# Splitting the right operands of a Strassen-style matmul kernel two k-tiles at a time

## The chip, the cores and the metric

The kernel runs on one core of a Trainium2 chip (trn2). The core's engines each work through a queue of their own, in order, and meet at semaphores: TensorE (PE) does the matmuls, VectorE (DVE) and ScalarE (ACT) the elementwise work, GpSimd (POOL) a little at the start, SyncE (SP) issues the transfers. The metric is the device time of one execution in microseconds (us), median of the runs shown.

## What is computed

One layer on x of 1024 rows by 1024 features, all in float32: a gated mixer and a squared-ReLU MLP, each behind an RMS norm and with a residual.

```python
def gmlp_mixer(h, w_in, ln_g, w_s, b_s, w_out):
    z = jax.nn.gelu(h @ w_in)                     # 1024 -> 4096
    u, v = jnp.split(z, 2, axis=-1)
    ...                                           # layer norm of v, times ln_g
    v = v.reshape(b, l // CHUNK, CHUNK, GM_GROUPS, GM_GDIM)
    ws = jnp.where(causal[None], w_s, jnp.zeros_like(w_s))
    sv = jnp.einsum('gts,bnsge->bntge', ws, v) + b_s.T[None, None, :, :, None]
    return (u * sv.reshape(b, l, GM_WIDTH)) @ w_out

x = x + gmlp_mixer(rms_norm(x, norm1_g), ...)
x = x + jnp.square(jax.nn.relu(rms_norm(x, norm2_g) @ mlp_w1)) @ mlp_w2
return rms_norm(x, final_g)
```

## The kernel before

**Stages.** Every large product is cut into products of 1024x1024 by 1024x1024, and each of these is done by Strassen's scheme with seven products of 512x512 blocks instead of eight. Eight *single* stages n = 0 to 7 make the two v halves (n = 0, 1), the two u halves (2, 3) and the four parts of the MLP's hidden layer (4 to 7). Three *double* stages d = 0 to 2 take two such products at once into the same sums: w_out after stage 3, w2 after stage 7. A stage has seven positions, one for each product. The right operands are weight blocks b11 to b22, loaded as they are, or differences of them (T1 to T4, made by DVE at L1228 with `sum_t`).

**Split numbers.** A float32 operand is split into a high part (rounded to the fast type fp32r, by ACT) and a low part (the rest, by DVE), and a product is three matmuls: high by high, low by high, high by low (`products`, L387, L391, L392). A *unit* is one k-tile (128 of the 512 terms) of one position: 12 matmuls, three for each of four PSUM banks.

**The ring.** The left operands' parts stay in SBUF for the whole stage. The right operands' parts pass through a ring of four slots. In a single stage a slot holds one k-tile: `ring_high` and `ring_low`, each 128x512. `split_high` (L855) rounds a k-tile on ACT, once PE has finished the unit that had the slot; `split_low` (L1192) subtracts on DVE. The semaphores `high_done` and `low_done` count k-tiles, and PE waits for `low_done` before each unit. In a double stage a slot holds the left and the right operand of a unit, 128x1024 each of high and low: `pair_high` (L883), `pair_low` (L1200). Its first two slots lie where the ring's four lie, the other two in another region.

**Order.** The order on each engine is written out by hand in `single(n)` and `double(d)`: the four splits of every position are set down one at a time, and the other work stands between them: sums of the results in PSUM (`add_block`, L1309, four operations of 128x512), the T differences, sums for the next stage's left operand (`sum_s`, L1418), evictions and activations on ACT, and in stages 2 and 3 (the u halves) the gating. Gating a block takes a layer norm on ACT (`normalise`, L1001), 16 products of 128x128 in each of which the fp32 matmul runs as two (`mini`, L443) on PE, and eight operations on DVE (`gate`, L1357 and L1372). The names matter at position 5 of stages 2 and 3, where DVE's part of the order is:

```python
                split_low(n, 5, 0)
                split_low(n, 5, 1)
...
                if kind(n) == "u":
                    gate(n, "c11")
                sum_t(n, 3)
                split_low(n, 5, 2)
                if kind(n) == "u":
...
                    nc.vector.tensor_tensor(block_of["c12"], block_of["c12"], block_of["c22"], ALU.add)\
                      .then_inc(p5_added, 1)
                split_low(n, 5, 3)
```

The 128x2048 sum in it is L1523. At the end of a stage the first splits of the next one (`next_high`, `next_low`) stand between the last gates: the gate for c22 ahead of the third, the gate for c12 ahead of the fourth. In stage 1, two copies of the transposed gating weights (`ws_t`, L1496) follow the fourth split of position 3, and PE needs the banks that they empty within that position.

Of the kernel before, what the change touches and what calls it, by code (L numbers as in the profile page):

```python
# [5 lines left out]
F32 = mybir.dt.float32  # L6
F32R = mybir.dt.float32r
# [50 lines left out]
def unit(n, pos, k):  # L58

    return 4 * (7 * n + pos) + k + (56 if n >= 4 else 0)  # L60
# [56 lines left out]
def trunk(nc, x, norm1_g, norm2_g, mlp_w1, mlp_w2, final_g, a_w_in, a_ln_g, a_ws, a_bs, a_w_out, out):  # L117
# [8 lines left out]
    with ExitStack() as ctx:  # L126
        def at(name, shape, offset, dt=F32):
            return nc.alloc_sbuf_tensor_at(name, shape, dt, offset=offset)
# [49 lines left out]
        block_of = {"c11": rows[:, 0:4, 0:NB], "c12": rows[:, 0:4, NB:], "c21": rows[:, 4:8, 0:NB],  # L178
                    "c22": rows[:, 4:8, NB:]}

        ring_high = [at(f"ring_high{e}", [P, NB], ring_at + 4096 * e, F32R) for e in range(4)]
        ring_low = [at(f"ring_low{e}", [P, NB], ring_at + 4096 * e + 2048, F32R) for e in range(4)]
        pair_at = [ring_at, ring_at + HALF, region("a12"), region("a12") + HALF]
        pair_high = [at(f"pair_high{e}", [P, 2, NB], pair_at[e], F32R) for e in range(4)]
        pair_low = [at(f"pair_low{e}", [P, 2, NB], pair_at[e] + 4096, F32R) for e in range(4)]
# [193 lines left out]
        def _(pe):  # L379
# [6 lines left out]
            def products(bank, stat_high, stat_low, mov_high, mov_low, start, stop, begins):  # L386
                first = nc.tensor.matmul(ps[:, bank, :], stat_high, mov_high, start=start, stop=False,  # L387
                                         skip_group_check=True)
                if begins:
                    first.then_inc(unit_begun, 1)  # L390
                nc.tensor.matmul(ps[:, bank, :], stat_high, mov_low, start=False, stop=False, skip_group_check=True)  # L391
                last = nc.tensor.matmul(ps[:, bank, :], stat_low, mov_high, start=False, stop=stop,  # L392
                                        skip_group_check=True)
                if stop:
                    last.then_inc(full[bank], 1)

            def single_unit(n, pos, k):
                s = S_SINGLE[pos]
                if n in (0, 4):
                    if pos == 0:  # L400
                        pe.wait_ge(combo_low, (10 if n == 4 else 0) + k + 1)
                    elif k == 0:
                        pe.wait_ge(combo_low, combo_low_count(n, s))
                pe.wait_ge(low_done, unit(n, pos, k) + 1)
                e = k % 4
                for m in range(4):
                    bank = set_of(slot(n, pos))[m]
                    if k == 0:
                        begin_fill(("product", n, pos), bank)
                    c = slice(m * P, (m + 1) * P)  # L410
                    starts = pos in CHAIN_START or (pos == 5 and kind(n) == "u")
                    start, stop = k == 0 and starts, k == 3
                    if kind(n) == "v":
                        products(bank, high[s][:, k, c], low[s][:, k, c], ring_high[e][:, :], ring_low[e][:, :],
                                 start, stop, m == 0)
                    else:
                        products(bank, ring_high[e][:, c], ring_low[e][:, c], high[s][:, k, :], low[s][:, k, :],
                                 start, stop, m == 0)

            def double_unit(d, pos, k):  # L420
# [401 lines left out]
        def _(act):  # L822
# [12 lines left out]
            def right_place(n, pos):  # L835
                return quarter[places(n)[{0: "b11", 1: "b21", 2: "b21", 3: "b11", 4: "b12", 5: "b22", 6: "b21"}[pos]]]

            def split_high(n, pos, k):
                if pos == 7:
                    n, pos = n + 1, 0  # L840
                u = unit(n, pos, k)
                if u == 0:
                    act.wait_ge(first_landed, 16)
                else:
                    right_ready(n, pos)
                if n == 4 and pos == 0 and k < 2:
                    act.wait_ge(unit_begun, done(unit_double(0, 6, 6)))
                elif n == 4 and pos == 0:
                    filled(act, ("double", 0, 6), set_of(slot_double(0, 6))[3])
                elif u >= 4 and k < 3:  # L850
                    act.wait_ge(unit_begun, done(u - 4))
                elif u >= 4:
                    before = (n, pos - 1) if pos else (n - 1, 6)
                    filled(act, ("product", *before), set_of(slot(*before))[3])
                nc.scalar.activation(ring_high[k][:, :], right_place(n, pos)[:, k, :], ACT.Copy)\  # L855
                  .then_inc(high_done, 1)

            def split_pair_high(d, pos, k):
                if pos == 7:
# [316 lines left out]
        def _(dve):  # L1176
# [8 lines left out]
            def right_place(n, pos):  # L1185
                return quarter[places(n)[{0: "b11", 1: "b21", 2: "b21", 3: "b11", 4: "b12", 5: "b22", 6: "b21"}[pos]]]

            def split_low(n, pos, k):
                if pos == 7:
                    n, pos = n + 1, 0  # L1190
                dve.wait_ge(high_done, unit(n, pos, k) + 1)
                nc.vector.tensor_tensor(ring_low[k][:, :], right_place(n, pos)[:, k, :],  # L1192
                                        ring_high[k][:, :].bitcast(F32), ALU.subtract).then_inc(low_done, 1)

            def split_pair_low(d, pos, k):
                if pos == 7:
# [513 lines left out]
```

## Time and profile before

| | before |
|---|---|
| median of 3 runs | 1149.25 us (1149.21 to 1150.16) |
| the profiled execution | 1149.28 us, span of its profile 1147.6 us |
| PE busy | 1126.0 us, 98% |
| DVE busy | 773.2 us, 67% |
| ACT busy | 561.4 us, 49% |
| granted TensorE clock, mean | 0.994 |

The span runs from the first to the last instruction of the profile; times in its views count from its start. An engine's busy time is a sum over stages; what it hides is seen in the waits of the engine that is busy nearly always, here PE, and in the order of time around them. In a timeline an entry in brackets gives the idle time of the engine before the row and the instruction that ended it.

### The profile page before, as it was taken

How to read it: one execution, taken by the hardware profiler on the slowest of the kernel's cores; microseconds unless marked ns; L12 is line 12 of the kernel's file. 1: busy time of each engine (PE TensorE's matmuls, PEld its weight loads, DVE VectorE, ACT ScalarE, POOL GpSimd, SP SyncE). 2: the span in 40 equal slices, each digit the busy share in tenths (PEclk: the TensorE clock that was granted, in tenths of full speed). 3: DMA queues.
4: the chain of work that ended last, by engine and by line, in shares of the span. 5: the costliest groups of instructions: out<-in, count | busy, mean ns of one | idle time of the engine just before them, and what ended most of it. 6: DMA issues, size and time to landing. Idle time of an engine off the chain costs nothing.

```text
span 1147.6 us, 13154 instructions
## 1 busy us (share of the span) xinstructions
PE 1126.0 (98%) x5155; PEld 937.4 (82%) x5155; DVE 773.2 (67%) x830; ACT 561.4 (49%) x855; POOL 19.6 (2%) x16
## 2 busy tenths in 40 slices
PE   9999999999999999999999999999999999999995
PEld 8888888888888788888888888888887888888884
DVE  6886655478678976657657547465587675676666
ACT  8663434553553334656664365455643343434443
POOL 5000000000000000000000000000000000000000
PEclk9999999999999999999999999999999999999998
DMA  8054253272965493331353635527858454242313
GB/s 330 1 183 147 74 184 110 74 251 80 330 236 205 167 334 142 146 111 37 110 184 115 216 111 194 195 107 275 293 220 304 153 203 183 110 177 80 110 37 146
DMA packets 74621, 191.17 MB, mean 167 GB/s; under 512 B 3104, under 2 KB 4160, under 8 KB 67904
## 3 DMA queue, kind: packets, MB, share of 16 engines
q1 hardware_dynamic: 74496, 190.33, 46.2%
q8 instruction: 40, 0.66, 0.2%
q14 instruction: 21, 0.17, 0.0%
q10 hardware_dynamic: 64, 0.02, 0.0%
HBM read 131.61 MB, written 58.72 MB: 166 GB/s over the span
## 4 chain that ended last, share of the span: by engine, by line
PE 88%; DVE 5%; issue 2%; DMA 2%; ACT 2%; POOL 1%; DVEq 0%; SPq 0%; ACTq 0%; POOLq 0%
PE banks L387 28%; PE banks L391 28%; PE banks L392 28%; PE banks L443 2%; DVE pair_low L1200 1%; POOL rows L1675 1%; DMA rows<-y_blocks 1%; PE banks L479 1%; DVE left_and_right L1249 1%; PE banks L450 1%; DMA rows<-in_x_dram 1%; DVE rows L1632 1%; DVE rows L1332 1%; DVE rows L1372 0%; ACT spare L1012 0%
## 5 line engine op out<-in xcount | busy, mean ns | idle before, releaser
L883 ACT ACTIVATE pair_high<-left_and_right 128x1024 fp32r<-128x1024 f32 x168 | 177.6, 1061 | 268.0 <-PE banks L387 215.5
L1192 DVE TENSOR_TENSOR ring_low<-left_and_right,ring_high 128x512 fp32r<-128x512 f32 x224 | 152.6, 689 | 214.5 <-ACT ring_high L855 214.1
L1200 DVE TENSOR_TENSOR pair_low<-left_and_right,pair_high 128x1024 fp32r<-128x1024 f32 x168 | 203.0, 1220 | 122.5 <-ACT pair_high L883 122.4
L855 ACT ACTIVATE ring_high<-left_and_right 128x512 fp32r<-128x512 f32 x224 | 139.4, 630 | 272.8 <-PE banks L387 174.7
L387 PE MATMUL banks<-pair_high 128*128 128x512 f32 x672 | 263.2, 392 | 3.4 <-DVE pair_low L1200 3.3
L391 PE MATMUL banks<-pair_low,pair_high 128*128 128x512 f32 x672 | 262.4, 390 | 0.0
L392 PE MATMUL banks<-pair_high,pair_low 128*128 128x512 f32 x672 | 262.1, 390 | 0.0
L387 PEld LDWEIGHTS banks<-pair_high 128*128 128x128 f32 x672 | 126.5, 188 | 31.3 <-DVE pair_low L1200 4.5
L387 PE MATMUL banks<-s_high,ring_high 128*128 128x512 f32 x384 | 149.6, 390 | 0.0
L391 PE MATMUL banks<-s_low,ring_high 128*128 128x512 f32 x384 | 149.5, 389 | 0.0
L392 PE MATMUL banks<-s_high,ring_low 128*128 128x512 f32 x384 | 149.5, 389 | 0.0
L392 PEld LDWEIGHTS banks<-pair_high,pair_low 128*128 128x128 f32 x672 | 126.6, 188 | 26.4
L391 PEld LDWEIGHTS banks<-pair_low,pair_high 128*128 128x128 f32 x672 | 126.6, 188 | 25.8
L387 PE MATMUL banks<-a_high,ring_high 128*128 128x512 f32 x288 | 112.8, 392 | 0.6 <-DVE scratch L1357 0.5
L392 PE MATMUL banks<-a_high,ring_low 128*128 128x512 f32 x288 | 112.2, 389 | 0.0
L391 PE MATMUL banks<-a_low,ring_high 128*128 128x512 f32 x288 | 112.1, 389 | 0.0
L392 PEld LDWEIGHTS banks<-s_high,ring_low 128*128 128x128 f32 x384 | 72.1, 188 | 15.0
L391 PEld LDWEIGHTS banks<-s_low,ring_high 128*128 128x128 f32 x384 | 72.1, 188 | 14.8
L387 PEld LDWEIGHTS banks<-s_high,ring_high 128*128 128x128 f32 x384 | 72.1, 188 | 14.8
L1228 DVE TENSOR_TENSOR left_and_right<-left_and_right 128x2048 f32<-128x2048 f32 x32 | 73.1, 2286 | 1.1
L387 PEld LDWEIGHTS banks<-a_high,ring_high 128*128 128x128 f32 x288 | 54.1, 188 | 12.4 <-DVE scratch L1357 1.5
L392 PEld LDWEIGHTS banks<-a_high,ring_low 128*128 128x128 f32 x288 | 54.1, 188 | 11.3
(101 smaller groups left out, 1213.1 us busy)
## 6 DMA issues: line engine op xcount, KB each, us to landing
left_and_right<-sums SPq DMA_DIRECT2D x40, 1024.0 KB, 7.3
left_and_right<-in_mlp_w_dram SPq DMA_DIRECT2D x36, 1024.0 KB, 6.3
sums<-rows SPq DMA_DIRECT2D x34, 1024.0 KB, 5.0
left_and_right<-in_a_w_in_dram SPq DMA_DIRECT2D x19, 1024.0 KB, 6.3
v_blocks<-rows SPq DMA_DIRECT2D x8, 1024.0 KB, 4.8
left_and_right<-in_a_w_out_dram SPq DMA_DIRECT2D x8, 1024.0 KB, 11.0
spare<-v_blocks SPq DMA_DIRECT2D x6, 1024.0 KB, 5.8
sums<-spare SPq DMA_DIRECT2D x6, 1024.0 KB, 3.9
```

Source lines behind the costliest of these rows:

```text
L387: first = nc.tensor.matmul(ps[:, bank, :], stat_high, mov_high, start=start, stop=False, skip_group_check=True)
L391: nc.tensor.matmul(ps[:, bank, :], stat_high, mov_low, start=False, stop=False, skip_group_check=True)
L392: last = nc.tensor.matmul(ps[:, bank, :], stat_low, mov_high, start=False, stop=stop, skip_group_check=True)
L443: mm = nc.tensor.matmul(ps[:, banks[m], c * P:(c + 1) * P], held[:, c, m * P:(m + 1) * P], ws_t[:, g, :], start=True, stop=True)
L450: nc.tensor.matmul(ps[:, 0, 0:P], ident[:, :], ident[:, :], start=True, stop=True)
L479: tr = nc.tensor.transpose(ps[:, banks[k], c * P:(c + 1) * P], rows[:, 4 * tb + c, f:f + P], ident[:, :])
L855: nc.scalar.activation(ring_high[k][:, :], right_place(n, pos)[:, k, :], ACT.Copy)\
L883: nc.scalar.activation(pair_high[(k + 2) % 4][:, :, :], pair_of(d, pos, k), ACT.Copy)\
L1192: nc.vector.tensor_tensor(ring_low[k][:, :], right_place(n, pos)[:, k, :], ring_high[k][:, :].bitcast(F32), ALU.subtract).then_inc(low_don ...
L1200: nc.vector.tensor_tensor(pair_low[e][:, :, :], pair_of(d, pos, k), pair_high[e][:, :, :].bitcast(F32), ALU.subtract).then_inc(low_done, 1)
L1228: nc.vector.tensor_tensor(*args, ALU.subtract).then_inc(t_summed, 1)
L1249: nc.vector.tensor_tensor(*args, ALU.subtract).then_inc(t_summed, 1)
```

## The change

In the single stages the right operand is rounded and subtracted for two k-tiles at once, in one 128x1024 operation on each engine, and the ring becomes two pairs in the tiles that the double stages use. A pair is made at the place in the order where its second k-tile was made (k odd); the call for the first k-tile does nothing any more. `high_done` and `low_done` go up by two. Only the very first position (stage 0, position 0) keeps single k-tiles. ACT's wait before a pair is the one that the second k-tile had. The double stages aren't touched.

```diff
-        ring_high = [at(f"ring_high{e}", [P, NB], ring_at + 4096 * e, F32R) for e in range(4)]
-        ring_low = [at(f"ring_low{e}", [P, NB], ring_at + 4096 * e + 2048, F32R) for e in range(4)]
         pair_at = [ring_at, ring_at + HALF, region("a12"), region("a12") + HALF]
...
             def single_unit(n, pos, k):
                 s = S_SINGLE[pos]
+                right_high, right_low = pair_high[k // 2][:, k % 2, :], pair_low[k // 2][:, k % 2, :]
...
-                        products(bank, high[s][:, k, c], low[s][:, k, c], ring_high[e][:, :], ring_low[e][:, :],
+                        products(bank, high[s][:, k, c], low[s][:, k, c], right_high, right_low,
                                  start, stop, m == 0)
...
             def split_high(n, pos, k):
...
+                first = (n, pos) == (0, 0)
+                if k % 2 == 0 and not first:
+                    return
                 u = unit(n, pos, k)
...
                 elif u >= 4:
                     before = (n, pos - 1) if pos else (n - 1, 6)
                     filled(act, ("product", *before), set_of(slot(*before))[3])
-                nc.scalar.activation(ring_high[k][:, :], right_place(n, pos)[:, k, :], ACT.Copy)\
-                  .then_inc(high_done, 1)
+                if first:
+                    nc.scalar.activation(pair_high[k // 2][:, k % 2, :], right_place(n, pos)[:, k, :], ACT.Copy)\
+                      .then_inc(high_done, 1)
+                else:
+                    nc.scalar.activation(pair_high[k // 2][:, :, :], right_place(n, pos)[:, k - 1:k + 1, :], ACT.Copy)\
+                      .then_inc(high_done, 2)
...
             def split_low(n, pos, k):
...
+                if k % 2 == 0 and not first:
+                    return
                 dve.wait_ge(high_done, unit(n, pos, k) + 1)
...
+                else:
+                    nc.vector.tensor_tensor(pair_low[k // 2][:, :, :], right_place(n, pos)[:, k - 1:k + 1, :],
+                                            pair_high[k // 2][:, :, :].bitcast(F32), ALU.subtract)\
+                      .then_inc(low_done, 2)
```

How the order on DVE changes, at the two kinds of places that the prediction speaks of. Names: `ring_low_79` to `_82` are the four slots, `pair_low_79` and `_80` the two pairs; line numbers after the diff are 15 higher, or 14 for the subtraction.

DVE in stage 2, from the second split of position 5 to the `add_block` after its last, before:

```order
L1192 TENSOR_TENSOR ring_low_80<-left_and_right,ring_high_76 128x512
L1357 SCALAR_TENSOR_TENSOR scratch<-banks,gains,bias 128x512 x2
L1372 TENSOR_TENSOR rows<-scratch,rows 128x512
L1357 SCALAR_TENSOR_TENSOR scratch<-banks,gains,bias 128x512
L1372 TENSOR_TENSOR rows<-scratch,rows 128x512
L1357 SCALAR_TENSOR_TENSOR scratch<-banks,gains,bias 128x512
L1372 TENSOR_TENSOR rows<-scratch,rows 128x512 x2
L1228 TENSOR_TENSOR left_and_right<-left_and_right 128x2048
L1192 TENSOR_TENSOR ring_low_81<-left_and_right,ring_high_77 128x512
L1523 TENSOR_TENSOR rows<-rows 128x4x512
L1192 TENSOR_TENSOR ring_low_82<-left_and_right,ring_high_78 128x512
L1309 TENSOR_TENSOR rows<-banks,rows 128x512 x4
```

and now:

```order
L1206 TENSOR_TENSOR pair_low_79<-left_and_right,pair_high_75 128x1024
L1372 SCALAR_TENSOR_TENSOR scratch<-banks,gains,bias 128x512 x2
L1387 TENSOR_TENSOR rows<-scratch,rows 128x512
L1372 SCALAR_TENSOR_TENSOR scratch<-banks,gains,bias 128x512
L1387 TENSOR_TENSOR rows<-scratch,rows 128x512
L1372 SCALAR_TENSOR_TENSOR scratch<-banks,gains,bias 128x512
L1387 TENSOR_TENSOR rows<-scratch,rows 128x512 x2
L1243 TENSOR_TENSOR left_and_right<-left_and_right 128x2048
L1538 TENSOR_TENSOR rows<-rows 128x4x512
L1206 TENSOR_TENSOR pair_low_80<-left_and_right,pair_high_76 128x1024
L1324 TENSOR_TENSOR rows<-banks,rows 128x512 x4
```

The third k-tile's subtraction, which stood ahead of the large sum, is now part of the one behind it.

DVE in stage 1, position 3, around the copies of the gating weights, before:

```order
L1192 TENSOR_TENSOR ring_low_81<-left_and_right,ring_high_77 128x512
L1228 TENSOR_TENSOR left_and_right<-left_and_right 128x2048
L1192 TENSOR_TENSOR ring_low_82<-left_and_right,ring_high_78 128x512
L1496 COPY ws_t<-banks 128x512 x2
L1192 TENSOR_TENSOR ring_low_79<-left_and_right,ring_high_75 128x512
```

and now:

```order
L1206 TENSOR_TENSOR pair_low_79<-left_and_right,pair_high_75 128x1024
L1243 TENSOR_TENSOR left_and_right<-left_and_right 128x2048
L1206 TENSOR_TENSOR pair_low_80<-left_and_right,pair_high_76 128x1024
L1511 COPY ws_t<-banks 128x512 x2
L1206 TENSOR_TENSOR pair_low_79<-left_and_right,pair_high_75 128x1024
```

Ahead of the copies a subtraction of 128x512 has become one of 128x1024.

## Rows read from the trace of the kernel before

**Rows 1.** The page: busy time, share of the span and instructions of each engine.

```profile
PE 1126.0 (98%) x5155; PEld 937.4 (82%) x5155; DVE 773.2 (67%) x830; ACT 561.4 (49%) x855; POOL 19.6 (2%) x16
```

**Rows 2.** The page's groups: count, busy us, mean ns of one, idle before.

```profile
L883 ACT ACTIVATE pair_high<-left_and_right 128x1024 fp32r<-128x1024 f32 x168 | 177.6, 1061 | 268.0 <-PE banks L387 215.5
L1192 DVE TENSOR_TENSOR ring_low<-left_and_right,ring_high 128x512 fp32r<-128x512 f32 x224 | 152.6, 689 | 214.5 <-ACT ring_high L855 214.1
L1200 DVE TENSOR_TENSOR pair_low<-left_and_right,pair_high 128x1024 fp32r<-128x1024 f32 x168 | 203.0, 1220 | 122.5 <-ACT pair_high L883 122.4
L855 ACT ACTIVATE ring_high<-left_and_right 128x512 fp32r<-128x512 f32 x224 | 139.4, 630 | 272.8 <-PE banks L387 174.7
```

**Rows 3.** PE's waits: for whom, us in total, times, longest.

```profile
PE banks L387 <- DVE pair_low L1200: 3.3, 3, 2.1
PE banks L479 <- POOL rows L1675: 2.2, 1, 2.2
PE banks L443 <- ACT spare L1001: 1.6, 1, 1.6
```

**Rows 4.** Timeline of DVE, stage 2, position 5: start, duration, row.

```profile
229.98 0.69 DVE L1192 TENSOR_TENSOR ring_low<-left_and_right,ring_high 128x512 fp32r<-128x512 f32 x1 [5.25 <-ACT ring_high L855]
230.59 1.40 DVE L1357 SCALAR_TENSOR_TENSOR scratch<-banks,gains,bias 128x512 f32<-128x512 f32 x2
...
236.01 2.29 DVE L1228 TENSOR_TENSOR left_and_right<-left_and_right 128x2048 f32<-128x2048 f32 x1
...
238.82 2.29 DVE L1523 TENSOR_TENSOR rows<-rows 128x2048 f32<-128x2048 f32 x1
241.02 0.68 DVE L1192 TENSOR_TENSOR ring_low<-left_and_right,ring_high 128x512 fp32r<-128x512 f32 x1
```

**Rows 5.** Timelines of ACT and PE there: second rounding, third k-tile's first matmul.

```profile
229.31 0.63 ACT L855 ACTIVATE ring_high<-left_and_right 128x512 fp32r<-128x512 f32 x1 [5.31 <-PE banks L387]
...
239.72 0.39 PE L387 MATMUL banks<-s_high,ring_high 128*128 128x512 f32 x1
```

**Rows 6.** The same of a common place, stage 6, position 5, first pair.

```profile
724.00 0.63 ACT L855 ACTIVATE ring_high<-left_and_right 128x512 fp32r<-128x512 f32 x1 [2.09 <-PE banks L387]
...
728.95 0.39 PE L387 MATMUL banks<-s_high,ring_high 128*128 128x512 f32 x1
```

**Rows 7.** Chain, PE's timeline, and windows: stretch, length, PE busy (count), clock, DMA.

```profile
882.37 1.14 DVE pair_low L1200
...
883.55 0.73 PE L387 MATMUL banks<-pair_high 128*128 128x512 f32 x1 [2.12 <-DVE pair_low L1200]
...
30.30:33.70 3.40, 3.40 (x18) 0.50 0.00 0
...
365.10:368.50 3.40, 3.40 (x30) 1.00 0.09 34
...
883.65:887.06 3.41, 3.41 (x8) 0.50 1.06 389
```

**Rows 8.** Timelines of ACT, DVE and PE, stage 1, position 3.

```profile
131.69 0.63 ACT L855 ACTIVATE ring_high<-left_and_right 128x512 fp32r<-128x512 f32 x1 [1.86 <-PE banks L392]
...
133.27 1.28 DVE L1496 COPY ws_t<-banks 128x512 f32<-128x512 f32 x2
...
134.00 0.50 PE L387 MATMUL banks<-ring_high,s_high 128*128 128x512 f32 x1 [0.15 <-DVE ws_t L1496]
```

**Rows 9.** Timelines of DVE and PE, end of stage 2 and start of stage 3.

```profile
261.96 1.40 DVE L1357 SCALAR_TENSOR_TENSOR scratch<-banks,gains,bias 128x512 f32<-128x512 f32 x2
...
266.33 0.50 PE L387 MATMUL banks<-a_high,ring_high 128*128 128x512 f32 x1 [0.49 <-DVE scratch L1357]
...
269.86 0.39 PE L387 MATMUL banks<-a_high,ring_high 128*128 128x512 f32 x1
```

**Rows 10.** Timelines of ACT and PE, start of stage 4.

```profile
518.20 1.15 ACT L855 ACTIVATE ring_high<-left_and_right 128x512 fp32r<-128x512 f32 x2 [1.85 <-PE banks L387]
...
520.43 0.39 PE L387 MATMUL banks<-a_high,ring_high 128*128 128x512 f32 x1
```

More of the change, by code:

```diff
@@ L404, in single_unit @@
                 pe.wait_ge(low_done, unit(n, pos, k) + 1)
-                e = k % 4
                 for m in range(4):
@@ L413, in single_unit @@
                     if kind(n) == "v":
-                        products(bank, high[s][:, k, c], low[s][:, k, c], ring_high[e][:, :], ring_low[e][:, :],
+                        products(bank, high[s][:, k, c], low[s][:, k, c], right_high, right_low,
                                  start, stop, m == 0)
                     else:
-                        products(bank, ring_high[e][:, c], ring_low[e][:, c], high[s][:, k, :], low[s][:, k, :],
+                        products(bank, right_high[:, c], right_low[:, c], high[s][:, k, :], low[s][:, k, :],
                                  start, stop, m == 0)
@@ L1190, in split_low @@
                     n, pos = n + 1, 0
+                first = (n, pos) == (0, 0)
+                if k % 2 == 0 and not first:
+                    return
                 dve.wait_ge(high_done, unit(n, pos, k) + 1)
-                nc.vector.tensor_tensor(ring_low[k][:, :], right_place(n, pos)[:, k, :],
-                                        ring_high[k][:, :].bitcast(F32), ALU.subtract).then_inc(low_done, 1)
+                if first:
+                    nc.vector.tensor_tensor(pair_low[k // 2][:, k % 2, :], right_place(n, pos)[:, k, :],
+                                            pair_high[k // 2][:, k % 2, :].bitcast(F32), ALU.subtract)\
+                      .then_inc(low_done, 1)
+                else:
+                    nc.vector.tensor_tensor(pair_low[k // 2][:, :, :], right_place(n, pos)[:, k - 1:k + 1, :],
+                                            pair_high[k // 2][:, :, :].bitcast(F32), ALU.subtract)\
+                      .then_inc(low_done, 2)
             def split_pair_low(d, pos, k):
```

## The prediction, made before the changed kernel was run

> **What bounds the kernel now.** I read first the busy line of the page: PE is busy 98% of the span, VectorE (DVE) 67%, ScalarE (ACT) 49% [rows 1]. So DVE and ACT matter only where PE waits for them. The list of PE's waits names few: 3.3 us in three waits for the double stages' subtraction, 1.6 us for a normalisation [rows 3]; none for a single stage's `ring_low`. Whatever the change saves on DVE and ACT in the single stages is therefore hidden already, and the question is whether every right operand still arrives in time. For that I read timelines of DVE, ACT and PE around each of the 112 places where a single stage needs its first or third k-tile, then the windows with the granted clock.
>
> **What the change removes and adds.** The first four k-tiles keep their single operations. The other 220 roundings (630 ns each) become 110 of 128x1024, and 220 subtractions (689 ns) become 110. The kernel already runs both larger forms in the double stages: 1061 and 1220 ns [rows 2]. Busy time: ACT 220 x 0.630 - 110 x 1.061 = 22 us less, DVE 220 x 0.689 - 110 x 1.220 = 17 us less. Both are hidden, so they count 0; if they weren't hidden they could only shorten waits of PE, and those of the single stages come to under 1 us in all apart from the start. Matmuls, loads and stores stay. PE reads the larger tiles in the double stages at the same 390 ns per matmul, so I take 0 for the new layout.
>
> **What it moves.** The pair is made where the second of its two k-tiles was made. Before, a slot was freed after one unit (12 matmuls at 0.227 us, 2.72 us) and had three units until it was needed. Now the first k-tile of a pair waits until both of the old ones are used, and has two units, 5.44 us, for rounding, subtraction and whatever stands ahead of them on the in-order queues. A common place: the second k-tile's rounding starts at 724.00 and PE begins the pair at 728.95 [rows 6]. With the pair: 724.00 + 1.06 + 0.03 = 725.09 for the start of the subtraction, 1.18 until PE can start (a pair subtraction that began at 882.37 let PE go at 883.55 [rows 7]), so ready at 726.27, 2.7 us to spare. SP's loads wait for the count after the fourth k-tile; that moves by about 1 us, and the weights aren't used until a position or more later: 0.
>
> The rule for the rest is simple: a pair is ready about when the second k-tile was ready before, plus 0.43 us on ACT and 0.53 us on DVE, less one small operation (0.6 us) where the first k-tile's stood between. I compared this with PE's need at every pair. It fails in these places.
>
> **Position 5 of stages 2 and 3, third k-tile: the main term.** DVE's order is subtraction 2, eight gate operations, the 128x2048 difference of T4, subtraction 3, the 128x2048 sum at L1523, subtraction 4. Before: the gate began at 230.59 after a subtraction started at 229.98, T4 at 236.01, the sum at 238.82, subtraction 4 at 241.02 [rows 4]. PE began the third k-tile at 239.72 [rows 5], just after subtraction 3 (done 238.9). Now subtraction 3 is part of the one that stands last. Step by step: ACT begins at 229.31 as before (released by PE, which has just passed the small gating matmuls [rows 5]); 229.31 + 1.06 + 0.03 = 230.40; the pair's subtraction holds DVE 1.14 us, to 231.54; gate 236.01 - 230.59 = 5.42, to 236.96; T4 (236.01 to 238.82 without the 0.60 of subtraction 3) 2.21, to 239.17; sum 2.20, to 241.37; PE goes 1.18 later, at 242.55. Against 239.72 that is a wait of **2.83 us**. The pattern stands twice, the second time 91.72 us later in stage 3: 5.7 us. Nothing takes it back: DVE, ACT and SP behind it are released by PE, and the waits of the double stages (at 363, 396 and 881) lead back to PE's own progress.
>
> **The clock after these waits.** The trace has two cases on either side. After a wait of 2.12 us PE ran the next 3.41 us at a granted clock of 0.50, that is at 1.2 instead of 2.4 GHz [rows 7]; the same followed a wait of 2.2 us near 28 [rows 3, 7]. After the wait of 1.6 us at 363.5 [rows 3] the clock stayed at 1.00 [rows 7]. A wait of 2.83 us lies above both cases that lost the clock, so I take it for each. At half clock 8 matmuls stand in 3.41 us [rows 7], 0.43 each; at full clock the 15 from 266.33 to 269.86 take 0.23 each [rows 9], so 8 take 1.8: a loss of 1.6 us each, 3.2 in all. Bounds: 0 (neither) to 3.2 (both).
>
> **The small places.** Stage 1, position 3: PE waits at 134.00 for a copy of the transposed gating weights that DVE began at 133.27, after subtraction 4 [rows 8]. The pair's rounding starts at 131.69, its subtraction at 132.78 and ends its hold at 133.92, so the copy moves by 0.65: +0.6 us. Stage 2 to 3: the two gates now stand together ahead of the second pair. The first is 0.96 later (as above), the second, before at 261.96, has lost a subtraction in front: 0.96 - 0.60 = +0.36, and PE's wait at 266.33 for its bank grows by as much: +0.4 us. The pair then begins after the second gate (5.42 us from 262.32) at 267.75 and is ready at 268.93, before PE's 269.86 [rows 9]. Stage 4, position 0: ACT begins at 518.20, released by PE; 518.20 + 1.06 + 0.03 + 1.18 = 520.47 against PE's need at 520.43 [rows 10]: 0.04 and some 0.2 for a first matmul that was not prefetched, +0.2. Each fresh wait also costs about 0.1 us more in its first matmul, +0.2 for the two long ones. Places with some 0.1 to 1 us left (stage 0 above all) count 0; were three of them missed by a few tenths, +1.
>
> **Sum.** 5.7 + 3.2 + 0.6 + 0.4 + 0.2 + 0.2 = 10.3 us. The profiled execution took 1149.28 us around a span of 1147.6; the median is 1149.25, so nothing has to be corrected: 1149.3 + 10.3 = **1159.6 us**, 0.9% slower.
>
> **A rule of the notes.** DVE is busy 67% over the whole span, but without a pause from 229.98 to beyond 241.02 [rows 1, 4], 11 us. The Trainium skill, Perfetto Trace Analysis, section Optimizing Scalar/DVE Operations, says that grouping into larger operations can improve throughput if the engine is saturated, and that where it isn't saturated but makes bubbles elsewhere, breaking up lets work be completed sooner. By its first half, with DVE taken as saturated in that stretch, the change helps there; by its second it hurts. The rows decide for the second: grouping saves 2 x 0.61 - 1.14 = 0.08 us of DVE there, and what PE waits for comes 3.6 us later.
>
> **Rivals.**
> 1. The waits come, but the clock isn't lost after both (what is needed for it is seen at two waits only, and these lie elsewhere in the trace): one lost 1158.0, none lost 1156.4.
> 2. More places miss: the pairs of stage 0 and of stage 4 with under 1 us left. Against it: I worked each out with something to spare. 1161 to 1163.
> 3. Not slower: PE's wait at position 5 doesn't open, because the pair is ready by 239.72. That needs DVE to be 2.83 us earlier in the stretch. The one source is the grouping itself, which gives 0.08 us per pair; the point from which it decides is a gate and two large operations in under 7.0 us together, and they take 9.8. Then the small places alone would be left, +1.2 us: 1150.5, no difference.
> 4. Faster: DVE and ACT with 39 us less to do reach the double stages sooner, and the three waits for the pair subtraction (3.3 us) with the lost clock behind the last (1.6) go: 1149.3 - 4.9 = 1144.4. Against it: those waits lie in code that isn't changed, one behind a transfer.
> 5. The change doesn't do what it says: the order of instructions shows that it does; nothing is given to it.
>
> **How the numbers follow.** The forecast with both clocks lost 0.52, rival 1 0.31, rival 2 0.09, rival 3 0.05, rival 4 0.03. A measurement of this kernel can tell about 0.2%, 2.3 us, from no change. Slower by more than that are the first three, 0.92; within it 0.05; faster 0.03. The range takes rival 1 whole, with 1 us below it for terms sized too large, and most of rival 2: 1155.4 to 1162.6.
>
> **What would show it.** PE's waits for the single stages' `pair_low`: two of 2.8 us (this is the step on which all rests), near 240 and 336; after each a granted clock of 0.50 for 3.41 us; DVE busy about 756 and ACT about 539 us; the wait for `ws_t` about 0.8 us; the waits near 363, 396 and 881 in their old sizes, shifted by about 10 us. The prediction is wrong if no such wait stands at position 5, if the same opens in stages 4 to 7, or if a wait of the double stages shrinks by what these add.

## The result, and the profile after

| | before | changed |
|---|---|---|
| median | 1149.23 us (4 runs, 1148.2 to 1150.2) | 1159.76 us (4 runs, 1155.4 to 1163.2) |
| changed to before | | 1.009, 95% interval 1.005 to 1.013 |
| the profiled execution | 1149.28 us, span 1147.6 | 1155.40 us, span 1153.6 |
| DVE busy | 773.2 us | 761.8 us |
| ACT busy | 561.4 us | 544.1 us |

The changed kernel is 0.9% slower, with 10.5 us more in the median, and its executions lie 8 us apart where those of the kernel before lie 2 us apart. The profiled one is the fastest of the four. First the page of the changed kernel: busy time, and the groups of the new operations (count, busy us, mean ns, idle before).

```profile
PE 1124.2 (97%) x5155; PEld 933.1 (81%) x5155; DVE 761.8 (66%) x720; ACT 544.1 (47%) x745; POOL 19.5 (2%) x16
...
L1206 DVE TENSOR_TENSOR pair_low<-left_and_right,pair_high 128x1024 fp32r<-128x1024 f32 x110 | 134.9, 1226 | 234.6 <-ACT pair_high L861 234.6
...
L861 ACT ACTIVATE pair_high<-left_and_right 128x1024 fp32r<-128x1024 f32 x110 | 116.7, 1061 | 300.7 <-PE banks L385 209.3
L385 PE MATMUL banks<-s_high,pair_high 128*128 128x512 f32 x384 | 149.8, 390 | 5.7 <-DVE pair_low L1206 5.7
```

The operations cost what they cost in the double stages before [rows 2], the matmuls 390 ns as before, and DVE and ACT have less to do. PE's idle time has a new entry, 5.7 us in front of a single stage's matmuls. The list of PE's waits says how it is spread (total, times, longest):

```profile
PE banks L385 <- DVE pair_low L1206: 5.7, 2, 2.9
PE banks L385 <- DVE pair_low L1215: 3.9, 5, 2.1
PE banks L477 <- POOL rows L1690: 2.2, 1, 2.2
PE banks L441 <- ACT spare L1007: 1.6, 1, 1.6
...
PE banks L385 <- DVE ws_t L1511: 0.9, 1, 0.9
PE banks L385 <- DVE scratch L1372: 0.9, 2, 0.5
```

The first line isn't in [rows 3]: two waits. The place is the one forecast; DVE's timeline of stage 2, position 5 (compare [rows 4]), then ACT's and PE's (compare [rows 5]):

```profile
229.80 1.23 DVE L1206 TENSOR_TENSOR pair_low<-left_and_right,pair_high 128x1024 fp32r<-128x1024 f32 x1 [7.54 <-ACT pair_high L861]
230.94 1.40 DVE L1372 SCALAR_TENSOR_TENSOR scratch<-banks,gains,bias 128x512 f32<-128x512 f32 x2
...
236.37 2.29 DVE L1243 TENSOR_TENSOR left_and_right<-left_and_right 128x2048 f32<-128x2048 f32 x1
238.57 2.28 DVE L1538 TENSOR_TENSOR rows<-rows 128x2048 f32<-128x2048 f32 x1
240.77 1.22 DVE L1206 TENSOR_TENSOR pair_low<-left_and_right,pair_high 128x1024 fp32r<-128x1024 f32 x1
```

```profile
228.63 1.06 ACT L861 ACTIVATE pair_high<-left_and_right 128x1024 fp32r<-128x1024 f32 x1 [5.75 <-PE banks L385]
...
242.05 0.50 PE L385 MATMUL banks<-s_high,pair_high 128*128 128x512 f32 x1 [2.87 <-DVE pair_low L1206]
```

From the rounding at 228.63 to PE's start at 242.05 it is 13.42 us; the sum of the prediction had 242.55 - 229.31 = 13.24. DVE stops for no more than 0.1 us at a time between 229.80 and the end; PE stands for 2.87 us. Subtracting the start times of the same matmul in the two traces, place by place, gives the account without the clock, with the slower first matmuls: +0.8 us at ws_t, +3.2 at position 5 of stage 2, +0.5 at the gates, +3.15 in stage 3, +0.35 at stage 4: 8.0 us. From 31 us to the double stage near 890 no other place loses more than 0.1 us.

The spans differ by 6.0 only. The windows of PE show why (stretch, length, PE busy with count, granted clock, DMA share, GB/s); these are the stretches of the changed kernel behind its waits that begin near 28, 239, 335 and 888:

```profile
30.00:33.40 3.40, 3.36 (x23) 1.00 0.00 0
242.10:245.50 3.40, 3.40 (x15) 1.00 1.05 404
337.40:340.80 3.40, 3.40 (x15) 1.00 0.99 392
890.00:893.40 3.40, 3.08 (x13) 1.00 1.05 386
```

This execution never lost the clock, not after the two waits of 2.87 us and not near 30 and 883, where the kernel before had [rows 7]. That gives back 1.6 us near 30 and about 0.4 at 890 (two new waits of 0.3 us for DVE follow there, which half clock had covered): 8.0 - 2.0 = 6.0.

### The profile page after: what moved, and what is told of

It is laid out like the page before. It is cut to its first block, busy times and chain, and to the rows that moved or that the text cites. A ratio compares the mean times of both kernels' runs of the same rounds, so it can differ in the third digit from the quotient of the medians.

```text
span 1153.6 us, 12933 instructions
## 1 busy us (share of the span) xinstructions
PE 1124.2 (97%) x5155; PEld 933.1 (81%) x5155; DVE 761.8 (66%) x720; ACT 544.1 (47%) x745; POOL 19.5 (2%) x16
## 4 chain that ended last, share of the span: by engine, by line
PE 85%; DVE 7%; issue 2%; ACT 2%; DMA 2%; POOL 1%; DVEq 0%; SPq 0%; ACTq 0%
PE banks L385 28%; PE banks L390 27%; PE banks L389 27%; PE banks L441 2%; DVE pair_low L1215 1%; DVE left_and_right L1264 1%; DMA rows<-in_x_dram 1%; POOL rows L1690 1%; DMA rows<-y_blocks 1%; DVE rows L1387 1%; PE banks L477 1%; DVE rows L1647 1%; DVE rows L1347 1%; ACT spare L1018 0%; DVE pair_low L1206 0%
## 5 line engine op out<-in xcount | busy, mean ns | idle before, releaser
L889 ACT ACTIVATE pair_high<-left_and_right 128x1024 fp32r<-128x1024 f32 x168 | 177.6, 1060 | 267.8 <-PE banks L385 216.4
L1206 DVE TENSOR_TENSOR pair_low<-left_and_right,pair_high 128x1024 fp32r<-128x1024 f32 x110 | 134.9, 1226 | 234.6 <-ACT pair_high L861 234.6
L1215 DVE TENSOR_TENSOR pair_low<-left_and_right,pair_high 128x1024 fp32r<-128x1024 f32 x168 | 203.1, 1221 | 121.2 <-ACT pair_high L889 121.0
L861 ACT ACTIVATE pair_high<-left_and_right 128x1024 fp32r<-128x1024 f32 x110 | 116.7, 1061 | 300.7 <-PE banks L385 209.3
L385 PE MATMUL banks<-s_high,pair_high 128*128 128x512 f32 x384 | 149.8, 390 | 5.7 <-DVE pair_low L1206 5.7
L390 PE MATMUL banks<-s_high,pair_low 128*128 128x512 f32 x384 | 149.4, 389 | 0.0
L389 PE MATMUL banks<-s_low,pair_high 128*128 128x512 f32 x384 | 149.4, 389 | 0.0
L385 PE MATMUL banks<-a_high,pair_high 128*128 128x512 f32 x288 | 112.8, 392 | 1.0 <-DVE scratch L1372 0.9
L390 PE MATMUL banks<-a_high,pair_low 128*128 128x512 f32 x288 | 112.1, 389 | 0.0
L389 PE MATMUL banks<-a_low,pair_high 128*128 128x512 f32 x288 | 112.1, 389 | 0.0
L385 PEld LDWEIGHTS banks<-s_high,pair_high 128*128 128x128 f32 x384 | 72.1, 188 | 21.4 <-DVE pair_low L1206 6.6
L390 PEld LDWEIGHTS banks<-s_high,pair_low 128*128 128x128 f32 x384 | 72.1, 188 | 15.1
L390 PEld LDWEIGHTS banks<-a_high,pair_low 128*128 128x128 f32 x288 | 54.1, 188 | 11.4
## 6 DMA issues: line engine op xcount, KB each, us to landing
left_and_right<-in_a_w_out_dram SPq DMA_DIRECT2D x8, 1024.0 KB, 10.3
```

Of the source, the lines that this page charges most:

```text
L861: nc.scalar.activation(pair_high[k // 2][:, :, :], right_place(n, pos)[:, k - 1:k + 1, :], ACT.Copy)\
L889: nc.scalar.activation(pair_high[(k + 2) % 4][:, :, :], pair_of(d, pos, k), ACT.Copy)\
L1206: nc.vector.tensor_tensor(pair_low[k // 2][:, :, :], right_place(n, pos)[:, k - 1:k + 1, :], pair_high[k // 2][:, :, :].bitcast(F32), ALU. ...
L1215: nc.vector.tensor_tensor(pair_low[e][:, :, :], pair_of(d, pos, k), pair_high[e][:, :, :].bitcast(F32), ALU.subtract).then_inc(low_done, 1)
```

## The experiments

Every kernel ran beside the kernel before, whose median was 1149.6 us in each set. What the theory says: PE's loss is two waits at position 5, where a pair's subtraction stands behind a sum that the third k-tile had passed, and a clock that is sometimes lost behind them.

**1. Single k-tiles at that one place.**

```diff
-                first = (n, pos) == (0, 0)
+                first = (n, pos) == (0, 0) or (n in (2, 3) and pos == 5 and k >= 2)
```

> The changed kernel, but in stages 2 and 3 the third and fourth k-tile of position 5 are rounded and subtracted one at a time again; all other pairs stay. My theory (the loss comes from the two waits of 2.87 us at that one place, plus the clock that is sometimes lost behind them): both waits vanish, the ones at ws_t, at the gates and at stage 4 stay with 1.6 us together, so 1149.2 + 1.6 = 1150.8 us, and the runs lie within about 2 us of each other as those of the kernel before. Rival (pairs cost time everywhere, by less slack or by the layout): it stays above 1155.

Measured: 1153.44 us (1152.5 to 1153.9), ratio 1.0034 (1.0021 to 1.0047). The large waits are gone and with them the spread; 6.3 us of the median come back. The rival (above 1155) falls. But it isn't 1150.8. The list of PE's waits has an entry that I hadn't expected, and PE's timeline shows where its larger part is:

```profile
PE banks L385 <- DVE pair_low L1206: 1.0, 2, 0.5
```

```profile
247.50 0.50 PE L385 MATMUL banks<-a_high,pair_high 128*128 128x512 f32 x1 [0.49 <-DVE pair_low L1206]
```

It is the first pair of position 6, behind the add for c22: DVE is still late from the first pair of position 5 (by 0.96 us in the sum of the prediction). With a wait of 0.14 us at position 5 and the slower first matmuls it makes 1.3 us in each of the two stages, 2.6 in all. In the changed kernel PE's own wait at position 5 hides it.

**2. A pair at that one place alone.**

```diff
-                first = (n, pos) == (0, 0)
+                first = not (n in (2, 3) and pos == 5 and k >= 2)
```

> The kernel before in its operations, with the tiles of the changed one, and pairs only for the third and fourth k-tile of position 5 in stages 2 and 3 (two pairs in all). My theory: the wait is the same, since the sum stands ahead of the pair, though the second k-tile's single operations save 0.5 us ahead of it: 2.83 - 0.5 = 2.3 us per wait, 2.6 with the slower first matmuls, so 1149.2 + 5.2 = 1154.4 us with as many half-clock stretches as before, up to 1157.6 with two more. Rival (many small losses): under 1151.

Measured: 1155.56 us (1152.9 to 1157.0), ratio 1.005 (1.0036 to 1.0063). Two pairs out of 110 make over half of the loss, part of it by the clock; the rival (under 1151) falls. PE's rows in stage 2, and the windows behind the two waits (in each window PE, PEld, DVE, ACT and POOL stand ahead of the clock):

```profile
241.90 0.50 PE L385 MATMUL banks<-s_high,pair_high 128*128 128x512 f32 x1 [1.81 <-DVE pair_low L1206]
```

```profile
242.60:245.90 3.30, 3.30 (x10) 2.53 (x9) 2.84 (x5) 2.61 (x5) 0.00 (x0) 0.50 1.03 391
338.20:341.50 3.30, 3.30 (x9) 2.57 (x8) 2.67 (x5) 2.44 (x5) 0.00 (x0) 0.50 1.00 395
```

The wait is 1.81 and not 2.3 us, because the expectation took off only 0.5 us for the first pair of the position, which is single here; it had made 0.96 us of the delay: 236.01 + 2.21 + 2.20 + 1.18 = 241.60 by [rows 4], 1.88 behind 239.72. And a wait of 1.81 us lost the clock both times. The profiled execution is the slowest of the five, with a mean granted clock of 0.991; the fastest, 1152.9 us, had 0.996, which leaves no room for them.

**3. The sum behind the pair.** DVE's 128x2048 sum of position 5 changes places with the subtraction.

```diff
+                split_low(n, 5, 3)
                 if kind(n) == "u":
...
                     nc.vector.tensor_tensor(block_of["c12"], block_of["c12"], block_of["c22"], ALU.add)\
                       .then_inc(p5_added, 1)
-                split_low(n, 5, 3)
```

> The changed kernel with DVE's 128x2048 sum of position 5 (stages 2 and 3) moved behind the pair's subtraction. My theory: the pair is ready 2.20 us earlier, the wait falls from 2.87 to about 0.65 us, and the next pair (position 6) comes 0.2 us late behind the sum and the add: 0.9 us per stage. 1149.2 + 1.6 + 1.8 = 1152.6 us, no half clock behind such short waits, runs within 2 us. Rival (ACT or the transfer sets the pair's time): the wait stays near 2.9 and the time near 1159.

Measured: 1153.75 us (1152.0 to 1154.2), ratio 1.0034 (1.0021 to 1.0047). PE's waits for this subtraction:

```profile
PE banks L385 <- DVE pair_low L1206: 1.3, 2, 0.7
```

2.2 us of DVE work out of the way take 2.2 us off each wait: the pair's time is set by what stands ahead of it on DVE, and neither ACT nor a transfer has a part. The time is 1.1 us above the forecast one: 0.4 of it because I had started from 1149.2 and the kernel before ran at 1149.6 in this set; for the rest, by the start times in the trace each stage loses 1.3 us where 0.9 was forecast (0.9 at position 5, as there is the slower first matmul behind the wait of 0.66, and 0.4 at the first pair of position 6).

**4. A longer wait, for the clock.** Two additions of 128x1024 more on DVE ahead of the sum, results unused.

```diff
                 if kind(n) == "u":
+                    dve.wait_ge(gated, block_piece(n - 2, "c11", 3))
+                    for i in range(2):
+                        nc.vector.tensor_tensor(scratch[:, :, :].rearrange("p a b -> p (a b)"),
+                                                bias[:, :, :].rearrange("p g t -> p (g t)"),
+                                                bias[:, :, :].rearrange("p g t -> p (g t)"), ALU.add).then_inc(padded, 1)
+                        dve.wait_ge(padded, 2 * (n - 2) + i + 1)
```

> The changed kernel with two additions of 128x1024 more on DVE ahead of that sum (their results aren't used), in stages 2 and 3. The two waits grow from 2.87 to about 5.2 us: 4.7 us more. On the clock, theory A (whether half clock follows depends on the length alone, and 2.87 us is near the edge; 2.12 and 2.20 us lost it in one run and not in another, so this must be wide) against theory B (it depends on where the wait falls, and a wait long enough loses it always): both give half clock after each of the two here, 3.2 us; by B the runs then spread by the other places alone, 3 us at most, around 1149.2 + 8 + 4.7 + 3.2 = 1165 us. If neither holds, some runs come without it, near 1161, and the spread stays at 6 us or more.

Measured: 1166.91 us (1165.0 to 1167.5), ratio 1.0149 (1.0135 to 1.0163). The waits are 5.39 us each, and PE starts behind both at half clock:

```profile
245.61 0.80 PE L386 MATMUL banks<-s_high,pair_high 128*128 128x512 f32 x1 [5.39 <-DVE pair_low L1207]
```

```profile
242.50:249.20 6.70, 3.59 (x9) 0.50 1.04 393
344.90:348.20 3.30, 3.07 (x7) 0.50 1.05 403
```

The clock falls while PE still waits: at 242.42, 2.2 us into the first wait, for 6.83 us, of which PE works the last 3.6, and 0.3 us before the second wait ends. The longer stretch therefore costs hardly more than the other, 1.7 and 1.4 us by the start times. The four executions lie within 2.6 us, as forecast. Both theories forecast that, so this run doesn't tell one from the other, and only one of its executions has a profile. Of the 1.9 us above the forecast 0.4 are the start from 1149.2 and 0.3 the longer waits; the other 1.2 stay open.

**5. The changed kernel once more.** No edit.

> The changed kernel unchanged, for a second profile and more executions, because its four executions reached from 1155.4 to 1163.2 us and the profile is of the one without half clock. Theory B (a wait of 2 to 3 us loses the clock in some executions and not in others, by where it falls): waits of 2.87 us again, half clock behind one or both of them in this or not, and executions apart by steps of about 1.6 us, 1155 to 1163. Rival (something else makes the slow executions, a transfer or a longer wait): a profile of an execution near 1160 shows PE's waits longer than 2.9 us, not half-clock stretches.

Measured: 1159.85 us (1157.4, 1159.7, 1159.9, 1161.1, 1162.3), ratio 1.0094 (1.0079 to 1.0110). The profiled execution took 1159.72 us. Its waits at position 5 are the same 2.87 and 2.86 us, and this time the clock is lost behind both:

```profile
339.96 0.73 PE L385 MATMUL banks<-s_high,pair_high 128*128 128x512 f32 x1 [2.86 <-DVE pair_low L1206]
```

```profile
244.50:247.90 3.40, 3.40 (x9) 2.65 (x8) 2.00 (x3) 3.40 (x7) 0.00 (x0) 0.50 1.06 398
340.10:343.40 3.30, 3.30 (x8) 2.60 (x9) 3.30 (x5) 2.60 (x5) 0.00 (x0) 0.50 1.01 406
```

Two executions of one program, equal waits at position 5, 1155.4 and 1159.7 us: 3.2 of the 4.3 us between them are the clock. Most of the rest comes from the first 11 us, where PE waits 0.8 us for DVE's scaling of the rows of x (0.3 in the other profile) and ends 0.9 us later. With 8.0 us for the waits, 3.2 for two half-clock stretches and 0.9 at the start, less 1.8 for the stretches near 30 and 883, which this execution too was spared, PE's later matmuls stand 10.3 to 10.4 us behind the kernel before. The rival (a longer wait) falls.

The executions without a profile have a mean granted clock too. From the fastest on, the nine of both sets have 0.996 (1155.40), 0.996 (1157.38), 0.995 (1157.60), 0.993 (1159.72 and 1159.85), 0.991 (1161.14) and 0.990 (1161.91, 1162.27 and 1163.18). The slower ones ran longer at half clock; the first two, 2.0 us apart at equal clocks, show that a part of the spread is something else.

**6. Pairs on ACT alone.** DVE subtracts one k-tile at a time, in the old order.

```diff
-                if k % 2 == 0 and not first:
-                    return
                 dve.wait_ge(high_done, unit(n, pos, k) + 1)
...
+                nc.vector.tensor_tensor(pair_low[k // 2][:, k % 2, :], right_place(n, pos)[:, k, :],
+                                        pair_high[k // 2][:, k % 2, :].bitcast(F32), ALU.subtract)\
+                  .then_inc(low_done, 1)
```

> The changed kernel with the subtraction on DVE one k-tile at a time again, in the old order; only ACT's rounding works on pairs. My theory (what is late is DVE's subtraction standing behind the sum; the later release and the longer rounding alone are covered): DVE starts only 0.43 us later behind each rounding, the third k-tile of position 5 is subtracted ahead of the sum again and ready at 239.4 against 239.72, so no wait of over 0.3 us there; 0.4 us more at the gates, 0.1 at ws_t: 1149.3 + 0.7 = 1150.0 us, runs within 2.5 us. Rival (the slot's later release is what hurts, three units of room against two): waits of over 2 us stay at position 5 and the time is above 1154.

Measured: 1157.51 us (1156.5 to 1157.9), ratio 1.0069 (1.0056 to 1.0081). At position 5 the forecast held (0.13 us), and the time was 7.5 us off all the same. By the start times of the matmuls 3.0 us are lost at `ws_t` in stage 1, where PE waits 3.1 us, 0.9 at a low part of the left operand in stage 0, 1.1 in each of stages 2 and 3 at positions 5 and 6, and 1.0 at the gates. DVE's timeline at `ws_t`:

```profile
129.24 1.28 DVE L1198 TENSOR_TENSOR pair_low<-left_and_right,pair_high 128x512 fp32r<-128x512 f32 x2
134.15 0.69 DVE L1198 TENSOR_TENSOR pair_low<-left_and_right,pair_high 128x512 fp32r<-128x512 f32 x1 [3.63 <-ACT pair_high L861]
134.76 2.28 DVE L1235 TENSOR_TENSOR left_and_right<-left_and_right 128x2048 f32<-128x2048 f32 x1
136.97 0.68 DVE L1198 TENSOR_TENSOR pair_low<-left_and_right,pair_high 128x512 fp32r<-128x512 f32 x1
137.57 1.28 DVE L1503 COPY ws_t<-banks 128x512 f32<-128x512 f32 x2
```

The third k-tile's subtraction stands in its old place, but its rounding now comes with the fourth's. DVE sits idle for 3.63 us in front of it, and then the difference and the copies come in one heap. In the changed kernel the subtraction has moved behind the difference, which fills that time. So the theory's side remark, that the later release alone is covered, is wrong: it holds at position 5 and fails elsewhere. The rival had the time right (above 1154) and the place wrong.

This wait also bears on the clock. It is longer than all those of the changed kernel, and the clock stayed at full speed behind it:

```profile
138.31 0.50 PE L385 MATMUL banks<-pair_high,s_high 128*128 128x512 f32 x1 [3.10 <-DVE ws_t L1503]
```

```profile
138.30:141.70 3.40, 3.40 (x15) 1.00 0.76 197
```

With 1.81 us that lost it twice in experiment 2, theory A (the length of the wait alone decides) falls.

**7. The later release by itself.** The kernel before, all operations single and in their old order; ACT's first and third rounding wait for what the second and fourth wait for.

```diff
-                elif u >= 4 and k < 3:
-                    act.wait_ge(unit_begun, done(u - 4))
+                elif u >= 4 and k < 2:
+                    act.wait_ge(unit_begun, done(u - k - 3))
```

> The kernel before with all its operations single and in their old order; only ACT waits, before the first and the third k-tile of a position, for the release of the second and the fourth, as with pairs. It tells the later release from the larger operations. My theory after the run with pairs on ACT alone: at position 5 no wait over 0.2 us; but DVE's first and third subtraction stand in their old places and now wait there, and what is queued behind them (T differences, ws_t copies, low parts of the left operand) comes late: some 2.7 us at ws_t in stage 1, 0.4 at s_low in stage 0, under 1 elsewhere: 1149.6 + 5 = 1154.5 us. Rival (the larger operation costs, not the release): under 1150.5.

Measured: 1160.57 us (1159.6 to 1161.5), ratio 1.0101 (1.0085 to 1.0116). The waits (total, times, longest):

```profile
PE banks L387 <- DVE s_low L1274: 3.6, 5, 0.8
PE banks L443 <- ACT spare L1001: 2.7, 2, 1.6
PE banks L387 <- DVE ws_t L1496: 2.7, 1, 2.7
```

With not one operation larger, the kernel is as slow as the changed one, but by other waits: at position 5 there is none. The 2.7 us at ws_t came as forecast; the low parts of stages 0 and 4 (four waits of 0.8 us, where I had given 0.4 us in stage 0 and under 1 elsewhere), a wait of 1.1 us for a normalisation and the clock once lost behind ws_t make the rest. The rival "the larger operation costs, not the release" falls here. What the run shows is that the later start of the first halves is costly where their old places are kept; it doesn't say that this made the changed kernel's waits, whose subtractions stand in other places.

**8. Pairs in an order that suits them.** In stages 2 and 3 the second pair of position 5 stands straight behind the gate, the first of position 6 ahead of the add for c22; the ws_t copies stand ahead of the pair, the gate for c22 ahead of stage 3's first pair, and position 0 of stage 4 keeps single k-tiles.

```diff
                     gate(n, "c11")
+                    split_low(n, 5, 3)
                 sum_t(n, 3)
...
+                if kind(n) == "u":
+                    split_low(n, 6, 1)
+                else:
+                    split_low(n, 5, 3)
                 add_block(n, "c22")
```

> The changed kernel with its pairs put where they are in time: in stages 2 and 3 the second pair of position 5 straight behind the gate (ahead of the T4 difference and the sum), the first pair of position 6 ahead of the add for c22; in stage 1 the ws_t copies ahead of the second pair of position 3; from stage 2 to 3 the gate for c22 ahead of the first pair; and position 0 of stage 4 with single k-tiles. My theory: by the times of the trace of before every pair is then ready before PE wants it, and the waits at the gates (0.63) and ws_t (0.15) of the kernel before go too: 1149.3 - 0.8 = 1148.5 us. Rival (work in pairs costs more than its order): 1151 or more.

Measured: 1152.47 us (1151.4 to 1156.4), ratio 1.003 (1.0019 to 1.0041). The rival's time came (1151 or more), but not its reason. No wait for a single stage's pair is left, and a new one stands in its place:

```profile
PE banks L441 <- DVE rows L1324: 3.9, 2, 2.0
```

The small gating matmuls after the second unit of position 6 need banks that DVE's add for c12 empties, and that add stood behind the second pair, whose rounding stood behind a normalisation on ACT until 248.69 in stage 2. So one more move, the add ahead of that pair:

```diff
+                if kind(n) == "u":
+                    add_block(n, "c12")
                 split_low(n, 6, 2)
                 split_low(n, 6, 3)
-                add_block(n, "c12")
+                if kind(n) != "u":
+                    add_block(n, "c12")
```

> The reordered version with one more move: in stages 2 and 3 the add for c12 stands ahead of the second pair of position 6 instead of behind it, since PE waited 1.97 us in each stage for the banks that this add empties. My theory: those two waits (4.2 us with the slower starts behind them) vanish, and the kernel with pairs everywhere costs the same as the kernel with single k-tiles in the same order: 1152.5 - 4.2 = 1148.3 us, within 1 us of the reordered kernel of before (1147.8). Rival (pairs cost more than their order): over 1150.

Measured: 1147.23 us (1146.4 to 1148.8), ratio 0.9982 (0.9974 to 0.9991). The first lines of PE's list now hold only what the kernel before had outside this matter (the double stages' waits with the 0.6 us that half clock had covered there):

```profile
PE banks L385 <- DVE pair_low L1215: 4.0, 5, 2.1
PE banks L477 <- POOL rows L1699: 2.2, 1, 2.2
PE banks L448 <- POOL ident L1704: 1.6, 1, 1.6
PE banks L441 <- ACT spare L1007: 1.6, 1, 1.6
```

**9. Two of these moves without pairs.** The kernel before, with the ws_t copies ahead of the fourth split and the gate for c22 ahead of stage 3's second.

> The kernel before, no pairs, with two of these moves: the ws_t copies ahead of the fourth split of position 3 in stage 1, and the gate for c22 ahead of the second split of stage 3's position 0. My theory: the gain of the reordered version belongs to the order, not to the pairs, so this one gives the same 1148.5 us. Rival (the saved 39 us of DVE and ACT are worth something once no pair is late): this one stays at 1148.5 and the reordered one with pairs is below 1147.

Measured: 1147.82 us (1147.0 to 1149.2), ratio 0.9989 (0.9980 to 0.9998). The version with pairs keeps DVE and ACT busy for 28 us less (762.0 and 544.5 us against 773.2 and 561.2) and is within 0.6 us of it; the intervals of the two ratios overlap. The gain over the kernel before, 1 to 2 us, belongs to the order: PE's two waits at the gates and the one at ws_t [rows 8, 9] are gone in both, and by the start times of the matmuls each of the two traces gains 0.4 us at ws_t and 1.0 at the gates.

## Why the prediction was right

- **Forecast 1159.6, measured 1159.76 and 1159.85.** So close a hit is partly luck, since the executions reach from 1155.4 to 1163.2, and since the sum leaves out that the kernel before's own two losses of the clock, near 30 and 883, can fail to come (2.0 us in the profiled execution); the range held both medians and eight of the nine executions; the slowest, 1163.18, lies above it.
- **The gain counted at nothing: right.** DVE and ACT lost busy time, and experiment 9 shows that it is worth nothing measurable even where no pair is late. The size by the page is 11.4 and 17.3 us, not 17 and 22: I multiplied mean durations, but an operation that follows another at once begins before the other's end (some 0.08 us on DVE, 0.11 on ACT [rows 10]), and the busy time counts that stretch once.
- **The wait at position 5: right in place and cause, nearly in size.** PE is idle for 2.87 us, twice. The forecast's 2.83 us was a difference of two start times, and so taken the two first matmuls come 3.03 us late. Two terms were too small. The subtraction began 1.17 us behind the rounding's start (229.80 - 228.63), not 1.09. PE started 1.27 us behind the subtraction's, not 1.18: the chain's row that I read [rows 7] begins where the operation before it ended, at 882.37, while by DVE's timeline that subtraction starts at 882.28. Experiments 1 to 3 took the wait away, made it alone and shortened it by the sum's 2.2 us.
- **The clock: right in size, by chance in number.** Each loss costs the 1.6 us of the sum. I gave both to the likeliest execution from two cases that lost it above 2.1 us; experiments 2, 5 and 6 show that the length doesn't decide in this range: 1.81 us lost it twice, 2.87 us lost it in one profile and not in the other, 3.10 us didn't lose it. Rival 1, with fewer losses, happened in some executions.
- **The small places: 1.6 us measured, 1.2 forecast**, and with the slower first matmuls 8.0 for all waits against 7.1. ws_t 0.8 (0.6), gates 0.5 (0.4), stage 4 0.35 (0.2), and 0.2 to 0.3 us more at each long wait than the 2.83 + 0.1 forecast, which are the two terms above; the 0.1 for a slower first matmul was right (its successor starts 0.34 us after it instead of 0.23). At stage 4 the sum's "some 0.2" for a first matmul was worked out from no row; the whole delay there measured 0.35, of which 0.12 are idle time.
- **Rival 2** (more places) didn't happen in the changed kernel; experiment 1 shows one that its long wait hides. **Rivals 3 and 4** fell: the waits of the double stages didn't shrink (3.9 us, 3.3 before; the 0.6 more is what half clock had covered).
- **The rule on breaking up.** The Trainium skill, Perfetto Trace Analysis, section Optimizing Scalar/DVE Operations, says that breaking up instructions may let work be completed sooner where the engines aren't saturated but cause bubbles elsewhere. The runs agree in experiment 1, where splitting two pairs brought back 6.3 us. Experiment 3 says what in the grouping cost: the sum of 2.2 us, which the first half used to pass and now stands behind. Experiment 8 (1147.23 us with pairs after the last move) shows that grouping costs nothing measurable once the order suits it.

## What to carry over

Before work on a ring is grouped, read for each slot when it is freed and when it is needed, and walk the in-order queue between the two with its durations: one large operation that the first half used to pass (here a 2.2 us sum) was enough, and over 100 of the 110 pairs were free. If grouped work stays where its last part stood, what stands between the parts goes ahead of it; if it's worth doing at all, the order has to be made anew, and each move can uncover the next wait. Time saved on engines that PE doesn't wait for isn't time saved.

## What was not expected of the hardware

- The granted clock fell to 0.50 for 3.41 us behind waits of PE of 1.81 us (twice), 2.12 to 2.23 (nine times) and 2.66 us, and did not fall behind others of 1.97 and 1.98 us (experiment 8, before the last move), 2.08 to 2.87 and 3.10 us, in equal programs even (2.87 us: twice lost, twice not, in two profiles). Behind 5.39 us it fell both times, while PE still waited, so that the longer stretch of 6.8 us cost only 1.7. Behind 1.56 us it fell in none of the twelve profiles. A wait in the middle range is thus a cost of 0 or 1.6 us by chance, and a kernel with more of them has executions that lie further apart: 2 us before, 8 us changed, most of it the clock. What decides between the two is not shown by these runs.
- Losing the clock can be cheaper than 1.6 us: at 883 the stretch at half clock covered two waits of 0.3 us for DVE, which appear in the profiles that kept the clock.
